# The four sums of a pair's weights: from GpSimd to VectorE, five products ahead

## What is computed

```python
# layer 0
proj = h @ w_in                                    # 1024 -> 6144
xa, ga, gb_post, gc_pre, v, gb = jnp.split(proj, EVEN_SPLITS, axis=-1)
ya = rg_lru(causal_dwconv(xa, conv_w, conv_b), w_a, b_a, w_x, b_x, lam)
yb = gb_post * causal_dwconv(gc_pre * v, sc_conv_w)
y = jnp.concatenate([ya * jax.nn.silu(ga), yb * jax.nn.silu(gb)], axis=-1)
# layer 1
proj = h @ w_in                                    # 1024 -> 4096
v, g = jnp.split(proj, 2, axis=-1)
pooled = jnp.stack([causal_window_mean(vg[:, :, k], POOL_WINDOWS[k])
                    for k in range(POOL_GROUPS)], axis=2)
mixed = jnp.einsum('bsgc,gcd->bsgd', pooled - vg, w_grp) + b_grp
y = mixed * scale * jax.nn.silu(g)
```

## Time and profile before

| | |
|---|---|
| median of 3 runs | 1356.64 us (1356.6 to 1356.75) |
| the profiled execution | 1361.12 us, of which the span from first to last instruction is 1359.3 us |
| TensorE busy | 1302.8 us, 96% of the span |
| VectorE busy | 951.6 us, 70% |
| ScalarE busy | 632.5 us, 47% |
| GpSimd busy | 318.7 us, 23% |
| mean granted clock of TensorE | 0.975 |

### The profile page before, as it was taken

How to read it: one execution, slowest core, us unless ns; L and a number is a source line. 1 busy time by engine, 2 the same in 40 slices (tenths; PEclk the granted TensorE clock), 3 DMA queues, 4 the chain that set the end, 5 groups by cost and what they waited for, 6 DMA issues and landing times.

```text
span 1359.3 us, 15668 instructions
## 1 busy us (share of the span) xinstructions
PE 1302.8 (96%) x5735; PEld 1071.8 (79%) x5735; DVE 951.6 (70%) x1118; ACT 632.5 (47%) x880; POOL 318.7 (23%) x190
## 2 busy tenths in 40 slices
PE   4998999999999999899999989998999999999997
PEld 4877788878887888688878868887887888888886
DVE  6888887878877796695667787747758647334554
ACT  6456456554646465333365554143143243223654
POOL 0024444534433332030300232132132130000000
PEclk7898999999999999999899989998999999999998
DMA  9911342323233242496738202320320321853463
GB/s 310 300 47 36 93 128 56 104 82 108 66 109 93 82 128 68 153 379 215 232 129 257 84 4 63 107 77 32 109 78 32 109 78 62 309 188 113 164 220 121
DMA packets 152864, 174.15 MB, mean 128 GB/s; under 512 B 7180, under 2 KB 115924, under 8 KB 152788
## 3 DMA queue, kind: packets, MB, share of 16 engines
q1 hardware_dynamic: 152788, 173.15, 39.6%
HBM read 143.76 MB, written 29.36 MB: 127 GB/s over the span
## 4 chain that ended last, share of the span: by engine, by line
PE 80%; DVE 11%; ACT 4%; issue 3%; DMA 1%; SPq 0%; ACTq 0%; DVEq 0%
PE psum L2062 26%; PE psum L2063 26%; PE psum L2064 26%; DVE X L1455 1%; DVE win L1925 1%; DVE w_lo L1365 1%; PE psum L2188 1%; PE psum L2380 1%; ACT w_hi L858 1%; DMA whole_x<-in_x 1%; ACT whole_x L1182 0%; DVE X L1461 0%; DVE w_lo L1388 0%; DMA raw<-in_hy_w_out 0%; DVE d_lo L1935 0%
## 5 line engine op out<-in xcount | busy, mean ns | idle before, releaser
L2062 PE MATMUL psum<-X,w_hi 128*128 128x512 f32 x1396 | 551.3, 395 | 21.9 <-DVE w_lo L1380 15.8
L2063 PE MATMUL psum<-X,w_hi 128*128 128x512 f32 x1396 | 547.1, 392 | 0.0
L2064 PE MATMUL psum<-X,w_lo 128*128 128x512 f32 x1396 | 546.8, 392 | 0.0
L2062 PEld LDWEIGHTS psum<-X,w_hi 128*128 128x128 f32 x1396 | 264.5, 189 | 84.6 <-issue 28.4
L2064 PEld LDWEIGHTS psum<-X,w_lo 128*128 128x128 f32 x1396 | 264.3, 189 | 55.6
L2063 PEld LDWEIGHTS psum<-X,w_hi 128*128 128x128 f32 x1396 | 264.5, 189 | 54.6 <-issue 0.5
L1365 DVE TENSOR_TENSOR w_lo<-raw,w_hi 128x1024 fp32r<-128x1024 f32 (+2 forms) x98 | 103.7, 1060 | 144.0 <-ACT w_hi L858 143.8
L858 ACT ACTIVATE w_hi<-raw 128x1024 fp32r<-128x1024 f32 (+2 forms) x98 | 89.6, 915 | 187.8 <-PE psum L2064 163.1
L881 ACT ACTIVATE w_hi<-ssum 128x512 fp32r<-128x512 f32 x140 | 86.8, 625 | 112.8 <-PE psum L2064 86.8
L1388 DVE TENSOR_TENSOR w_lo<-ssum,w_hi 128x512 fp32r<-128x512 f32 x140 | 115.9, 834 | 29.0 <-ACT w_hi L881 28.4
L810 POOL TENSOR_TENSOR ssum<-ssum,raw 128x512 f32<-128x512 f32 x35 | 54.7, 1562 | 305.3 <-DVE w_lo L1388 305.3
(11 more groups left out here) (240 smaller groups left out, 1858.4 us busy)
## 6 DMA issues: line engine op xcount, KB each, us to landing
raw<-in_hy_w_in SPq DMA_DIRECT2D x48, 512.0 KB, 5.1
raw<-in_pool_w_in SPq DMA_DIRECT2D x32, 512.0 KB, 5.2
bufs<-y_dram SPq DMA_DIRECT2D x48, 256.0 KB, 4.1
whole_x<-y_dram SPq DMA_DIRECT2D x48, 256.0 KB, 3.4
aux<-in_mod_w SPq DMA_DIRECT2D x16, 512.0 KB, 3.9
y_dram<-bufs SPq DMA_DIRECT2D x16, 512.0 KB, 2.7
raw<-in_hy_w_out SPq DMA_DIRECT2D x16, 512.0 KB, 5.6
raw<-in_mod_w SPq DMA_DIRECT2D x16, 512.0 KB, 5.1
```

Source lines behind the costliest of these rows:

```text
L2062: nc.tensor.matmul(out_, whi, xhi, start=first, stop=False, skip_group_check=check)
L2063: nc.tensor.matmul(out_, whi, xlo, start=False, stop=False, skip_group_check=check)
L2064: return nc.tensor.matmul(out_, wlo, xhi, start=False, stop=last, skip_group_check=check)
```

## The change

GpSimd's `sums_of_weights` is taken out. The four sums are made on VectorE, each by its own call `sum_of_weights(q, op)`, with the waits that GpSimd had. `prep(q, idx)` on VectorE now makes first the `lo` of three products ahead, as before, and then the sum of five ahead, if that operand is one of 2 to 5. `first_operands` makes the sums 2, 3 and 4 as well. GpSimd keeps `t1_and_t3`, the scaling of x by `std_bc`, and the eight small `tensor_scalar` that make `std_bc`, which stood one behind each of eight pairs' sums and now stand together ahead of them all, behind `t4_lo`. The loads, ScalarE's and TensorE's lists are as they were.

```diff
-            for q in range(3 * (HEADS - 1)):
-                sums_of_weights(q)
-                if 3 <= q < 3 + SB:
-
-                    b = q - 3
-                    pool.wait_ge(t4_lo, KP)
-                    nc.gpsimd.tensor_scalar(std_bc[:, b * P:(b + 1) * P], ident[:, :], sd[:, 0, b:b + 1], None,
-                                            ALU.mult).then_inc(diag0_ready, 1)
+            pool.wait_ge(t4_lo, KP)
+            for b in range(SB):
+
+                nc.gpsimd.tensor_scalar(std_bc[:, b * P:(b + 1) * P], ident[:, :], sd[:, 0, b:b + 1], None,
+                                        ALU.mult).then_inc(diag0_ready, 1)
...
-            for q in range(Q["V23", 0], len(PAIRS)):
-                sums_of_weights(q)
...
+            def sum_of_weights(q, op):
+
+                even, odd = (by_kp(ssum[:, n, :]) for n in range(2))
+                a11, a12 = (raw_blocks(q, 0)[:, n, :, :] for n in range(2))
+                a21, a22 = (raw_blocks(q, 1)[:, n, :, :] for n in range(2))
+                if op == 2:
+                    at = raw_at(("R2", q))
+                    dve.wait_ge(raw_in[at], raw_landed(("R2", q)))
+                    if q:
+                        dve.wait_ge(lo_done, HI["p", q - 1, 4])
+                    ins = nc.vector.tensor_tensor(even, a21, a22, ALU.add)
+                elif op == 3:
+                    at = raw_at(("R1", q))
+                    dve.wait_ge(raw_in[at], raw_landed(("R1", q)))
+                    if q:
+                        dve.wait_ge(lo_done, HI["p", q - 1, 5])
+                    dve.wait_ge(s_ready, 4 * q + 1)
+                    ins = nc.vector.tensor_tensor(odd, even, a11, ALU.add)
+                elif op == 4:
+                    dve.wait_ge(lo_done, HI["p", q, 2])
+                    dve.wait_ge(s_ready, 4 * q + 2)
+                    ins = nc.vector.tensor_tensor(even, odd, a12, ALU.add)
+                else:
+                    dve.wait_ge(lo_done, HI["p", q, 3])
+                    dve.wait_ge(s_ready, 4 * q + 3)
+                    ins = nc.vector.tensor_tensor(odd, a21, a11, ALU.add)
+                ins.then_inc(s_ready, 1)
+
             def prep(q, idx):
 
-                at = idx + 3
-                if at >= 7:
-                    q, at = NEXT.get(q), at - 7
-                if q is not None and at in OPERANDS:
-                    lo(q, at)
+
+                for ahead, make in ((3, lo), (5, sum_of_weights)):
+                    p, at = q, idx + ahead
+                    if at >= 7:
+                        p, at = NEXT.get(q), at - 7
+                    if p is not None and at in OPERANDS and (make is lo or at in (2, 3, 4, 5)):
+                        make(p, at)
 
             def first_operands(q):
                 lo(q, 0)
+                sum_of_weights(q, 2)
+                sum_of_weights(q, 3)
                 lo(q, 2)
+                sum_of_weights(q, 4)
```

More of the change, by code:

```diff
@@ L789, in _ @@
                                     pattern=[[-1, P]], channel_multiplier=1).then_inc(const_step, 1)
[L790 to L813, removed]
             def t1_and_t3(layer, kp):
```

## The result

| | before | changed |
|---|---|---|
| median of 8 runs | 1356.62 us (1354.77 to 1357.62) | 1368.10 us (1362.69 to 1373.51) |
| ratio | | 1.0087, interval 1.0067 to 1.0107 |
| profiled execution, its span | 1361.12, 1359.3 us | 1365.61, 1363.4 us |
| mean granted clock in it | 0.975 | 0.982 |

The change makes the kernel 11.5 us slower. The forecast was 1362.7, that is +6.1, with a range up to 1368.0: the sign was right, and the size forecast is half of the one measured.

What follows compares the result with a forecast made beforehand. TensorE, 96% busy, was taken as the bound, VectorE counting only where TensorE waits for it. The terms 4.3 + 0.9 + 1.1 + 1.6 + 0.8 - 1.35 - 1.65 + 0.45 gave +6.1 us, median 1362.7, range 1355.5 to 1368.

Steps and rivals of the forecast that it cites:

- The price of a sum: On VectorE, 0.60 us a sum, 0.72 behind the `lo` it waits on; 2.64 us a pair, 92 us for 35 pairs.
- the time given back: VectorE instructions no longer stretched by GpSimd's sums; 0.95 us back at each such `inputs_of_scan`.
- six ends of heads: Heads 1 to 6: sums ahead of `take_22` of pair C lengthen TensorE's wait, +4.3 us in all.
- pair A of head 4: `take_22` there had no idle in front and moves by 1.92 us, costing +0.9 us.
- Head 1's waits: Seven sums ahead of `take_22` of pair A, less stretches that go: net +1.1 us (0.7 to 1.5).
- the start of layer 1's pairs: The 5.20 us wait shrinks, but product "6" then waits for ScalarE's copy; -1.35 us remains.
- The cover at heads 1 and 4: VectorE's 0.96 us wait for product "3" ahead of `add_12` covers the rest, leaving +0.13 us each.
- The clock: Lower TensorE clock after longer idle: head 1 +1.6 us, head 5 +0.8 (half), head 3 0 (at most 1.6).
- Group 1 of layer 1: At G23 the wait at 939.40 falls, -1.65 us; group 2 the same, but then waits for `take_22`, +0.45 us.
- (a): Rival: time given back equals time taken also at ends of heads; 1356.6 us, within 0.2%; chance 0.22.
- (b): Rival: faster, layer 1's waits so short that the clock stays up, ends of heads at half; 1353 us; chance 0.10.
- (c): Rival: VectorE becomes the bound in the heads, `lo` of operand 0 late for product "1"; 1375 us; chance 0.13.

Runs made afterwards that it cites:

- ends_half: Kernel before, sums on GpSimd, with the `lo` of operand 2 of the next pair A made twice at the ends of heads 1 to 6; 1364.28 us, ratio 1.0048.
- again: The changed kernel run once more, nothing altered, for its own spread and a second trace; 1369.39 us, ratio 1.0086 to the kernel before.
- layer1_only: Changed kernel with only layer 1's sums (14 pairs) on VectorE, layer 0's left on GpSimd as before; 1359.38 us, ratio 1.0019.
- layer1_look: The kernel with only layer 1's sums on VectorE, run once more for a second trace; 1352.22 us, one execution.
- after_t22: Changed kernel with `take_22` of pair C moved ahead of `reset` and `inputs_of_scan` at the ends of heads 1 to 6; 1359.45 us, ratio 1.0017.
- late34: Changed kernel with sums 3 and 4 made behind `take_22` of the pair before, not ahead of it; 1354.92 us, ratio 0.9975.

## Why the prediction was half right

**The price of a sum, the time given back, the places.** Right. 0.60 and 0.72 us, 0.95 at each `inputs_of_scan`, and the six ends of heads and pair A of head 4 came out within 0.14 us each in the trace of the changed kernel. Head 1's waits were 1.08 and 1.07 for 1.1, the start of layer 1's pairs -1.51 and -1.57 for -1.35.

**The cover at heads 1 and 4.** The number held, 0.14 and 0.16 for 0.13; ends_half shows that it held because two of the three sums stand ahead of the wait for product "3".

**The clock. This is the step that failed.** The prediction took it as a step between 1.62 and 2.48 us of idle, each from one wait of one execution, gave head 3 (2.1) nothing "between the two" and head 5 half of its price. The runs show the full clock behind 2.12, 2.33, 2.62 and 3.04 us and the lower one behind 1.86, 2.11 and 2.60. So the length of the wait alone does not decide it: the same wait of the same kernel kept the clock in one execution and lost it in another, and a fall cost 1.3 to 2.9 us where no later wait covered it. Behind the copy in group 0 it fell in both traces of the changed kernel and cost nothing, since two waits of 0.89 and 0.21 us behind it, which the kernel before had, shrank or went. The change makes five new waits of 2 to 3 us (heads 3 and 5, the copy in group 0, G23 in groups 1 and 2) and lengthens that in head 1. Head 3 was mis-sized by up to 1.6, head 5 by 0.8 one way or the other, head 1 by up to 1.3, and groups 1 and 2 had no term for it. The clock term was 2.4 us in sum; the falls behind new or longer waits of `take_22` came to 5.8 us in the changed kernel's trace (2.93, 1.27, 1.60) and to 4.9 in "again" (1.65, 1.61, 1.63).

**Group 1 of layer 1.** The working stopped at the wait that falls, 3.81 to 2.23. Before, TensorE was at the lower clock behind it and so reached product "4" only at 944.7 us, long after `take_22`. With the clock up it gets there 2 us sooner and meets `take_22`, which three sums hold back, on VectorE of the changed kernel:

```profile
943.03 0.69 DVE L1359 TENSOR_TENSOR w_lo<-ssum,w_hi 128x512 fp32r<-128x512 f32 x1
943.75 0.69 DVE L1384 TENSOR_TENSOR ssum<-ssum,raw 128x512 f32<-128x512 f32 x1
944.36 1.22 DVE L1939 TENSOR_TENSOR d_lo<-vp,d_hi 128x1024 fp32r<-128x1024 f32 x1
945.50 0.68 DVE L1421 TENSOR_TENSOR gb_<-gb_,psum 128x512 f32<-128x512 f32 x1
```

The time up to that matmul is what was forecast (-1.58 - 2.24 + 2.06 = -1.8 for -1.65), but in two pieces of idle, and in the changed kernel's trace the clock fell behind the second, +1.27; in group 2 the same, +1.60. The prediction had this second wait in group 2 alone, and no clock behind it. In the other four traces with these sums on VectorE (again, layer1_only, layer1_look, after_t22) the clock fell behind the first wait of group 1 and stayed up behind the second. Yet in all five the time up to that matmul is 1.75 to 1.77 us less than before: VectorE sets it, so a fall behind the first wait costs nothing and a clock that stays up there gains nothing. A fall costs only behind the second.

**The sum.** The terms of idle were right within 0.5 us together. The trace of the changed kernel has 9.7 at the places of the prediction with the full clock at heads 3 and 5, "again" 8.3 with the lower clock there, but not behind the second waits of groups 1 and 2. With the lower clock at all of them it would be 9.7 + 1.6 + 1.6 = 12.9. The difference of the medians, 11.5, lies between, 5.4 above the forecast; of this the two traces show 3.6 and 2.2, nearly all of it clock; that the usual execution has most of these losses is worked out so, and no trace is of the median one.

**The rivals.** (a), that it evens out, fell at the ends of heads, where nothing came back but the 0.95. (b) needed the clock to stay up in group 1: it did in the changed kernel's trace, and the second wait took the gain of it; in "again" it did not, and the time up to product "4" was the same. (c) fell: no trace of the moved sums has a wait for `w_lo` inside heads 2 to 7.

## What to carry to other kernels

Work moved to an engine with 30% idle is paid at the few places where another engine waits for it: list them, and count each instruction put ahead of the one that releases. Look whether that one instruction can go first; here this gave 0.3% in the kernel before and 0.7% in the changed one, and with it, and with the sums 3 and 4 behind it, the choice of the engine made no difference that the intervals could settle. Where a change makes idle of some 2 us or more on TensorE, put a share of the clock's price on each such place, not none below a line and all above, and compare medians of many runs, since one trace shows one execution.

## What had not been expected of the hardware

- The granted clock fell behind 1.86 us of idle and stayed at 1.00 behind 2.33 within one execution, and stayed there behind 2.62 and 3.04 in another. Each fall that no later wait covered cost 1.3 to 2.9 us. The changed kernel, with more such waits, spread over 10.8 us in 8 runs and that of before over 2.9 in the 8 beside them (7.5 in 23 later ones), late34 over 2.7 in 12; but ends_half, with two such waits at ends of heads, spread over 3.0 in 6, so that the link of waits and spread is not shown for each kernel.
- Four GpSimd sums of 128x512 a pair cost the kernel 15 us of 1358. VectorE instructions of 0.68 and 1.22 us took up to 1.79 and 2.17 beside them, and at the ends of heads 3 and 5 the wait of TensorE fell by just that difference, 0.95 and 0.94, without the sums.
